# Three-branch attention with tokens on partitions: scores in two fp32r passes over stacked halves, probabilities as the stationary operand of the values' product, row sums divided out on the output

## The reference, cut to what matters

```python
def nsa_mixer(q, kc_raw, vc_raw, ks, vs, kw, vw, gates, pe, w1, w2, pos):
    q = rope(q), k_slc, k_win = rope(ks), rope(kw)
    p_cmp = safe_softmax(q @ k_cmp * 64 ** -0.5, compressed blocks that have ended)
    o_cmp = p_cmp @ v_cmp
    p = safe_softmax(q @ k_slc * 64 ** -0.5, mask);  o_slc = p @ v_slc
    p = safe_softmax(q @ k_win * 64 ** -0.5, mask);  o_win = p @ v_win
    return g[0] * o_cmp + g[1] * o_slc + g[2] * o_win
x = x + nsa_mixer(...) @ w_out
```

## Time and profile before

| | us |
|---|---|
| three runs | 4187.68, 4189.05, 4184.48; median 4187.68 |
| profiled execution, span (no other time of it is given) | 4191.9 |
| PE busy in the span | 3583.0 (85%) |
| PE weight loads | 2803.3 (67%) |
| DVE busy | 2293.2 (55%) |
| POOL busy | 1835.0 (44%) |
| ACT busy | 1449.5 (35%) |

### The profile page before, as it was taken

The page is one execution under the profiler, slowest core; times in us unless marked ns, Lnnn a source line. Parts: engine busy times, 40 slices in busy tenths (PEclk is TensorE's granted clock), DMA queues, the critical chain, the costliest instruction groups (busy, mean ns, idle before and its releaser), DMA issues. The chain is left out here.

```text
span 4191.9 us, 50533 instructions
## 1 busy us (share of the span) xinstructions
PE 3583.0 (85%) x16155; PEld 2803.3 (67%) x16159; DVE 2293.2 (55%) x3832; ACT 1449.5 (35%) x2631; POOL 1835.0 (44%) x986
## 2 busy tenths in 40 slices
PE   7778888745599999999998885889997779979997
PEld 4546576634488888888886653568776554457876
DVE  5976323887499999999995367421102326531101
ACT  4223332267633333333333232433212114433322
POOL 1521243178787888788883110134342200023432
PEclk9888999877799999999998897999998869999999
DMA  3121133012477777777772210123223130012321
GB/s 87 50 73 26 39 87 86 26 61 100 166 260 270 267 268 271 264 265 262 275 268 76 72 41 26 31 65 95 78 83 76 47 81 9 18 55 83 92 79 61
DMA packets 430765, 486.47 MB, mean 116 GB/s; under 512 B 61336, under 2 KB 373944, under 8 KB 412480
## 3 DMA queue, kind: packets, MB, share of 16 engines
q1 hardware_dynamic: 412224, 350.96, 27.8%
q0 software_dynamic: 18432, 134.23, 8.1%
HBM read 448.35 MB, written 29.36 MB: 114 GB/s over the span
## 5 line engine op out<-in xcount | busy, mean ns | idle before, releaser
L124 POOL TENSOR_TENSOR w_low<-w_ring,w_high 128x1024 fp32r<-128x1024 f32 (+2 forms) x264 | 650.4, 2471 | 1786.7 <-ACT w_high L119 1786.7
L129 PE MATMUL ps<-h_low,w_high 128*128 128x512 f32 x1600 | 657.3, 411 | 186.6 <-POOL w_low L124 133.1
L130 PE MATMUL ps<-h_high,w_high 128*128 128x512 f32 x1600 | 643.9, 402 | 0.0
L131 PE MATMUL ps<-h_high,w_low 128*128 128x512 f32 x1600 | 642.6, 402 | 0.0
L129 PEld LDWEIGHTS ps<-h_low,w_high 128*128 128x128 f32 x1600 | 309.5, 193 | 281.3 <-POOL w_low L124 148.6
L124 POOL TENSOR_TENSOR u_low<-w_ring,u_high 128x1024 fp32r<-128x1024 f32 x128 | 365.8, 2857 | 134.1 <-ACT u_high L119 133.6
L124 POOL TENSOR_TENSOR v_low<-v_raw,v_high 128x1024 fp32r<-128x1024 f32 x128 | 349.2, 2728 | 45.6 <-ACT v_high L119 45.6
L119 ACT ACTIVATE w_high<-w_ring 128x1024 fp32r<-128x1024 f32 (+2 forms) x264 | 263.1, 1012 | 301.5 <-PE ps L131 253.9
L130 PEld LDWEIGHTS ps<-h_high,w_high 128*128 128x128 f32 x1600 | 310.5, 194 | 72.9 <-issue 3.6
L131 PEld LDWEIGHTS ps<-h_high,w_low 128*128 128x128 f32 x1600 | 309.1, 193 | 73.5
L129 PE MATMUL ps<-h_low,u_high 128*128 128x384 f32 x1024 | 344.7, 337 | 6.5 <-POOL u_low L124 6.5
(11 more groups left out here) (395 smaller groups left out, 7063.7 us busy)
## 6 DMA issues: line engine op xcount, KB each, us to landing
w_ring<-in_peer_uT_dram SPq DMA_DIRECT2D x128, 512.0 KB, 5.2
v_raw<-in_peer_uv_dram SPq DMA_DIRECT2D x128, 512.0 KB, 4.3
peer_gates<-ring SPq DMA_DIRECT2D x12, 2048.0 KB, 6.2
gates<-peer_gates SPq DMA_DIRECT2D x32, 768.0 KB
w_ring<-in_ffn_w_gate_dram SPq DMA_DIRECT2D x44, 512.0 KB, 3.8
w_ring<-in_ffn_w_up_dram SPq DMA_DIRECT2D x44, 512.0 KB, 3.8
w_ring<-in_w_in_dram SPq DMA_DIRECT2D x36, 512.0 KB, 3.9
w_ring<-in_ffn_w_down_dram SPq DMA_DIRECT2D x32, 448.0 KB, 3.7
```

What stands on the lines that cost most here:

```text
L124: return eng.tensor_tensor(rounded(low), whole, high, ALU.subtract)
L129: nc.tensor.matmul(out, rounded(w_high), rounded(x_low), start=start, stop=False, **more)
L130: nc.tensor.matmul(out, rounded(w_high), rounded(x_high), start=False, stop=False, **more)
L131: return nc.tensor.matmul(out, rounded(w_low), rounded(x_high), start=False, stop=stop, **more)
```

## The change

It keeps what is computed and changes how, in four places.

`compressed` gets two more outputs: ACT makes 12 high halves (4 tiles of keys, 8 of queries, 128x512 each) at the head of its program in that stage, ahead of the copy of peT; POOL makes the 12 low halves behind its memset.

`nsa_attention` stacks halves on partitions: q's stack holds the 64 rows of the high half over the 64 rows of the low half of one head; the keys' two operands hold the high half twice, and the low half twice. A score is then two fp32r matmuls over 128 rows (all four products of halves). Staging takes two 64-partition copies for each of 8 q slots, 9 for each kind's keys and values, 2 for pc0 with vc, one for pc1: 37 in a turn instead of 11.

`attention_rows` replaces `attention` for this stage. Steps, lag, maxima, exps, masks, transposes and the split of copies over ACT (tiles 1, 3) and DVE (0, 2) stay. The probabilities are neither scaled nor gated. The transposes go through 3 banks in rotation. In `weigh` the transposed probabilities are stationary and 64 columns of values move: 10 matmuls a unit, and in kind 0 four more for the compressed branch, each kind into its own bank (6 and 7 by turns). A new `finish` on DVE, between the copy of tile 2 and the next step's maximum, does the reciprocal of the four row sums, the product with the gates, the scaling of the output [128, 4, 64], and its addition to the compressed part (kind 0) or to the rows so far (kind 1).

`project` gets `rows`: the output has tokens on partitions now, so PE transposes it, 4 transposes for each of 8 tiles into banks 4 to 7, and ACT and DVE take both halves from PSUM.

```diff
 def project(c, w, evacuate, ..., rows=None):
...
+    x_whole = (lambda k: whole[:, k, :]) if rows is None else (lambda k: c.ps[:, 4 + k % 4, :])
...
+            if rows is not None:
+                for k in range(KD):
+                    if k >= 4:
+                        pe.wait_ge(x_low, k - 3)
+                    for t in range(TT):
+                        tr = nc.tensor.transpose(c.ps[:, 4 + k % 4, t * P:(t + 1) * P], rows[:, t, k * P:(k + 1) * P], c.ident[:, :])
+                    tr.then_inc(x_turned, 1)
...
+                for k in range(x_tiles):
+                    if rows is not None:
+                        act.wait_ge(x_turned, k + 1)
+                    high_half(nc, rhs[0].high[:, k, :], x_whole(k)).then_inc(x_high, 1)
...
+def attention_rows(c, turns, units, staging, lag=3):
+    s_banks, pt_banks, out_banks = (0, 1, 2), (3, 4, 5), (6, 7)
...
+                def score(i, s):
...
+                    for x, (q, k) in enumerate(unit["scores"]):
+                        nc.tensor.matmul(c.ps[:, bank, 0:w], q[:, t * P:(t + 1) * P], k[:, 0:w], start=x == 0, stop=False)
...
+                def weigh(i, u):
+                    unit = units[u]
+                    for t in (act_tiles[-1], dve_tiles[-1]):
+                        moved(pe, i, TT * u + t)
+                    pe.wait_ge(o_read, i * n_units + (u + 1))
+                    for t in range(TT):
+                        tokens = slice(t * P, (t + 1) * P)
+                        for j in range(t + 1):
+                            mm = nc.tensor.matmul(out_of(u)[:, t, :], probsT[:, u % 2, j, tokens], unit["v"](j), start=j == 0, stop=j == t, skip_group_check=True)
+                        if "beside" in unit:
+                            weights, values = unit["beside"]
+                            mm = nc.tensor.matmul(out_of(u, 1)[:, t, :], weights[:, tokens], values, start=True, stop=True, skip_group_check=True)
+                    mm.then_inc(pv_done, 1)
...
+            @block.vector
...
+                    for s in range(n_steps + lag):
+                        if s < n_steps:
+                            u, t = steps[s]
+                            dve.wait_ge(scored, i * n_steps + (s + 1))
+                            nc.vector.tensor_reduce(top[...], c.ps[...], AX.X, ALU.max, negate=True).then_inc(topped, 1)
+                        if s >= lag and steps[s - lag][1] in dve_tiles:
+                            move(dve, i, s - lag, pt_dve, nc.vector.tensor_copy)
+                        if s >= lag and steps[s - lag][1] == 2 and steps[s - lag][0] >= 1:
+                            finish(steps[s - lag][0] - 1)
...
-def compressed(c, A, w, qT, kT, order, pcT, vcr):
+def compressed(c, A, w, qT, kT, order, pcT, vcr, q_halves, k_halves):
...
+        wholes = [(k_halves, x, kT[:, 2 + x, :]) for x in range(4)] + [(q_halves, x, qT[:, x, :]) for x in range(KD)]
...
             def _(pool):
                 nc.gpsimd.memset(hidden[:, :, :, :, :], 0.0).then_inc(padded, 1)
+                for n, (halves, x, whole) in enumerate(wholes):
+                    pool.wait_ge(split_high, n + 1)
+                    low_half(nc.gpsimd, halves.low[:, x, :], whole, halves.high[:, x, :]).then_inc(split_low, 1)
...
             def _(act):
+                for halves, x, whole in wholes:
+                    high_half(nc, halves.high[:, x, :], whole).then_inc(split_high, 1)
                 act.wait_ge(pe_turned, 1)
...
-def nsa_attention(c, qT, kT, vs, vw, order, pcT, vcr, oT):
+def nsa_attention(c, q_halves, k_halves, vs, vw, order, pcT, vcr, o_rows):
...
+        def q_stack(j, b):
+            return lambda i: [(q[j, b][HALF[x], :], q_halves[x][HALF[b], i * TILES + j, :]) for x in range(2)]
+
+        def kv(kind, buf):
+            return lambda i: [(k[kind, b][x][HALF[y], :], k_halves[x][HALF[b], i + 2 * kind, :])
+                              for b in range(2) for x in range(2) for y in range(2)] + [(v[kind][:, :, :], buf[:, :, bass.ds(i * P, P)])]
...
+            def finish(dve, i, out, beside, total):
...
+                nc.vector.reciprocal(gate, total).then_inc(turned, 1)
+                dve.wait_ge(turned, now)
+                nc.vector.tensor_tensor(gate, gate, order[...], ALU.mult).then_inc(gated, 1)
+                dve.wait_ge(gated, now)
+                nc.vector.tensor_tensor(one, out, gate.unsqueeze(2).to_broadcast([P, TT, NSA_D]), ALU.mult).then_inc(parted, 1)
+                dve.wait_ge(parted, now)
+                return nc.vector.tensor_tensor(dest, one, beside if kind == 0 else dest, ALU.add)
```

More of the change, by code:

```diff
@@ L337, in count, with project @@
         return False
-def project(c, w, evacuate, rhs=None, ahead=None, whole=None, before={}, after={}, norm=None):
+def project(c, w, evacuate, rhs=None, ahead=None, whole=None, before={}, after={}, norm=None, rows=None):
     nc = c.nc
@@ L353, in project @@
     mm_done, bank_free, high, low = (ctx.sem(n) for n in ("mm_done", "bank_free", "high", "low"))
-    x_high, x_low = ctx.sem("x_high"), ctx.sem("x_low")
+    x_turned, x_high, x_low = ctx.sem("x_turned"), ctx.sem("x_high"), ctx.sem("x_low")
     w_halves = c.halves(ctx, "w", [P, per_turn, max(w.kt) * P])
+    x_whole = (lambda k: whole[:, k, :]) if rows is None else (lambda k: c.ps[:, 4 + k % 4, :])
+    x_tiles = whole.shape[1] if whole is not None else KD if rows is not None else 0
     fresh = w.count(c)
@@ L414, in _ @@
                 before["pe"](pe)
-            if whole is not None:
-                pe.wait_ge(x_low, whole.shape[1])
+            if rows is not None:
[5 more added lines that the diff above has]
+                    tr.then_inc(x_turned, 1)
+            if x_tiles:
+                pe.wait_ge(x_low, x_tiles)
             def body(i):
@@ L447, in start @@
             def start():
-                if whole is not None:
-                    for k in range(whole.shape[1]):
-                        high_half(nc, rhs[0].high[:, k, :], whole[:, k, :]).then_inc(x_high, 1)
+                for k in range(x_tiles):
+                    if rows is not None:
+                        act.wait_ge(x_turned, k + 1)
+                    high_half(nc, rhs[0].high[:, k, :], x_whole(k)).then_inc(x_high, 1)
             if "act" not in evacuate:
@@ L491, in _ @@
                 before["dve"](dve)
-            if whole is not None:
-                for k in range(whole.shape[1]):
-                    dve.wait_ge(x_high, k + 1)
-                    low_half(nc.vector, rhs[0].low[:, k, :], whole[:, k, :], rhs[0].high[:, k, :]).then_inc(x_low, 1)
+            for k in range(x_tiles):
+                dve.wait_ge(x_high, k + 1)
+                low_half(nc.vector, rhs[0].low[:, k, :], x_whole(k), rhs[0].high[:, k, :]).then_inc(x_low, 1)
             if "dve" in evacuate:
@@ L530, in project_copy, with project_add @@
     project(c, w, {"act": act}, ahead=ahead, before=before, after=after, norm=norm)
-def project_add(c, w, dest, rhs, whole=None, ahead=None, before={}):
+def project_add(c, w, dest, rhs, whole=None, ahead=None, before={}, rows=None):
     nc = c.nc
@@ L541, in dve @@
             nc.vector.tensor_tensor(d, d, c.ps[:, b, :], ALU.add).then_inc(bank_free, w.parts)
-    project(c, w, {"dve": dve}, rhs, ahead, whole, before)
+    project(c, w, {"dve": dve}, rhs, ahead, whole, before, rows=rows)
 def project_swiglu(c, w, gain, dest, ahead=None):
@@ L2429, in odd_mix @@
         c.h = c.halves(ctx, "h", [P, KD, T])
[L2430 removed]
+        o_rows = ctx.sbuf("o_rows", [P, TT, KD, P])
         with c.stage() as ctx:
[L2432 to L2433 removed]
+            k_halves = c.halves(ctx, "k", [P, 4, T])
             vs, vw = (ctx.sbuf(n, [P, TT, GW]) for n in ("vs", "vw"))
@@ L2629, in head @@
-        def head(j, b, kind):
-            half = slice(64 * b, 64 * b + 64)
-            unit = dict(q=q[j][half, :], k=lambda i: k[kind][half, :], v=lambda x: v[kind][:, x, half], mask=None,
-                        slots=[f"q{j}", f"kv{kind}"] + ["pc0", f"pc{j // 2}"][:1 + j // 2] * (kind == 0),
-                        gate=lambda i, t: order[:, t, 1 + kind, bass.ds(i * (2 * TILES) + (2 * j + b), 1)],
-                        out=c.ps[half, 7, :], sum=c.ps[:, 7, :], first=kind == 0, last=kind == 1)
+        stat = ctx.sbuf("stat", [P, 2, TT])
@@ L2636, in head @@
             if kind == 0:
                 rows = slice(32 * (2 * (j % 2) + b), 32 * (2 * (j % 2) + b) + 32)
-                unit["add"], unit["add_to"] = vc[rows, :], lambda i: pc[j // 2][rows, :]
+                unit["beside"] = pc[j // 2][rows, :], vc[rows, :]
             return unit
-        attention(c, KD // TILES, [head(j, b, kind) for j in range(TILES) for b in range(2) for kind in range(2)], 1.0, staging,
-                  {4 * j + 3: (lambda i, j=j: tile_of(oT, i, TILES, j)) for j in range(TILES)})
+        attention_rows(c, KD // TILES, [head(n, kind) for n in range(len(heads)) for kind in range(2)], staging)
```

170 lines of the change are left out of this document (146 added, 24 removed).

## The result

| | before | after |
|---|---|---|
| median of the runs, us | 4188.4 (4 runs) | 4252.3 (4 runs, 4243.9 to 4252.9) |
| ratio | 1 | 1.0147 (1.0135 to 1.0160) |
| profiled span, us | 4191.9 | 4251.2 |

The change costs 64 us (1.5%). I forecast slower, and +145. The profiled execution of the kernel before lay 3.5 us above its median, so the two spans differ by 59.3.

A forecast was written before the change was run, and what follows sets the result against it. No engine bounds the whole kernel; PE, busy throughout attention, was taken to run it at 1.2 GHz. Attention +122, staging +11.8, compressed stage +5.6, projection +4.4, last finish +0.7 make +145, so 4333 us; 8-in-10 range 4205 to 4375.

The forecast's parts named there:

- rival D: Attention: clock alternates because some stretch of new scores or products raises it; half the excess over rival B, some 4270; chance 0.14.
- The step that failed: Attention: all of it at 1.2 GHz, a pair 23.3 us, 16 pairs 373 instead of 240 us.
- The window's values: Window unit's weighing: 10 products of 2 instructions, 0.213 us each, 4.27 us in all at 1.2 GHz.
- The four scores of a unit: Attention unit: four fp32r scores take 3.53 us at 1.2 GHz, was 5.47.
- The score of 128 columns: Narrowest score: priced like the plain product, 2x0.43 us; bounds for a pass 0.11 and 0.43.
- The compressed part: Selected unit: compressed product becomes 4 products of 2 instructions, 8x0.213 = 1.71 us.
- rival B: Attention: clock rises and stays, DVE's finish chain of 4.6 plus weighing 2.4 bounds a unit at 7.0 us: 4210; chance 0.13.
- the cover of the finish: Attention units: DVE's finish, 1.2 us, hidden because PE needs 6.5 us between weighings and the chain under 5.
- Staging: Ahead of attention: SP issues copies at 0.63 to 0.76 us each, vc now the 25th, first score +11.8 us.
- Compressed stage: Stage before attention: 12 high halves on ACT ahead of peT's copy, +5.6 us; low halves on POOL at nothing.
- Output projection: After attention: ACT's split of oT waits for PE's transposes, +4.4 us; the last finish adds +0.7.
- Rival C: Attention: clock high, finish slips in while PE weighs, PE decides; 35 saved, 22 given back: 4175; chance 0.08.

The follow-up runs named there:

- e10: Changed kernel with score passes over only the 64 high-half rows of q, products with q's low half left out: 4349.8 us, ratio 1.0382.
- e6: e4 with q padded by zeros, so the plain fp32 scores run over 128 rows: 4233.8 us, ratio 1.0107.
- e4: Changed kernel with scores and staging put back to the earlier plain fp32 form; values, finish and output stay new: 4387.8 us, ratio 1.0474.
- e9: Changed kernel with the selected unit's compressed products moved out of its value weighing, finish left in place: 4235.6 us, ratio 1.0108.
- e13: e9 plus eight unread fp32r matmuls of 256 columns in the idle time ahead of the window weighing: 4193.9 us, ratio 1.0014.
- e7: Changed kernel with staging copies issued from two queues, SP and POOL: 4251.8 us, ratio 1.0143.
- e5: e1 with the selected unit's compressed products also moved out of its value weighing: 4161.7 us, ratio 0.9935.
- e12: e5 with the copy order of e11 and ACT's high halves moved behind the copy of peT: 4142.1 us, ratio 0.9882.
- e11: Changed kernel with only SP's staging order altered, the first unit's slots first: 4243.9 us, ratio 1.0134.
- e3: Kernel before with only the new scores, their splitting and staging; values and output in the old form: 4179.2 us, ratio 0.9972.
- e1: Changed kernel with the finish one step later on DVE, behind the fourth tile's maximum: 4206.6 us, ratio 1.0038.

## Why the prediction was right or wrong

The direction and the range for 8 in 10 (4205 to 4375) held, the latter because D and B widened it; my own range, 4292 to 4375, and the size did not: +64 for +145. What happened is rival D, which I gave 0.14 and priced at 4270.

- **The step that failed** is "What is left, loads and short streams in turn, looks like the stretches that stayed at 0.50. I therefore take the whole new attention at 1.2 GHz." The stretch that I took for the likeness, has its scores over 64 rows ("64*128" in the row); the new scores are stacked over 128. e10 and e6 show that this is the difference: over 64 rows 4350 us, near my 4333, over 128 rows 4252; and e4's 4388 against e6's 4234. I had read the columns of the rows and not the rows of the operand. The one term was worth 16 x (23.3 - 17.65) = 90 us, more than the whole miss of 81. That e10 comes so near to 4333 is in part luck, as the next point shows.
- **The steps inside it**, read from e10, which is slow all through. The window's values cost 0.215 us an instruction, forecast 0.213. The four scores of a unit take 3.44 us (0.61, 0.73, 0.94, 1.16), forecast 3.53, by two errors that cancel. The score of 128 columns is 0.43 shorter than my 1.04 (0.85 and 0.19): its fp32r pass is one and not four, since the second pass begins 0.27, 0.39, 0.49 and 0.59 us behind the first for 128 to 512 columns, in even steps. I took the wrong end of my bounds, 0.43 where 0.11 was the other. The wide ones sum to 2.83 where I had 1.92 + 3 x 0.19 = 2.49, so their loads are not hidden as in the earlier trace rows. The compressed part was too cheap by 0.77 us (8 x 0.31 against 1.71). The price of 0.213 is near what these products take apart from the values (1.90 us for 8 at 1.2 GHz in e9, 3512.63 to 3514.53); what I had at nothing is the mixing.
- **The chain of rival B** held: 4.6 forecast, 4.61 measured, though its parts were off by up to 0.12 both ways, and the window unit at 2.4 GHz is 6.83 for B's 7.0. I named it as what would stand if the cover of the finish went. It went, for 24.5 us of waiting ahead of the selected weighings and 12.1 ahead of the window's. The nearest run to B, e13, took 4194 us for B's 4210, which left out the 5.9 us of waits for staging that my own sum has.
- **Why D's price was 18 too high.** "Half the excess over B" rested on my pair of 23.3. The pair that is slow all through is 24.2 (e10), so that was not too dear. But the measured one has the low clock for less than half of it: some 6.5 of 17.65 us in the pair above, in the selected weighing and the scores behind it.
- **Staging:** first score +12.0, forecast +11.8. The waits for the window keys were 3.7 and 3.6, forecast 2.6 and 1.7; the boundary 2.2, forecast 3.2. The mechanism was wrong in part: I took SP's issue as the limit, and two queues do not halve it (e7).
- **Compressed stage:** PE got peT 5.9 us later, forecast 5.6, but only +3.7 arrived at the stage's end, at a mean clock of 0.59 against 0.57. The 60.4 it is held against is the longer of the stage's two lengths (56.3 in e4); against the shorter one it is +7.8. What decides between the two was not tried.
- **Output projection:** from the end of the last product of values to the first of the projection 13.3 us against 9.5, +3.9, forecast 4.4 + 0.7.
- **Rival C** (faster, PE bound, 4175) describes e5 and e12 (4162 and 4142 us), whose finish stands elsewhere. Its saving of 1.07 us a unit on scores was 1.25 (0.41, 0.63, 0.84, 1.05 us from the narrowest to the widest before; 0.29, 0.35, 0.46, 0.58 after, at 2.4 GHz).

Left open: e11's 8 us are not all in its own place, as its compressed stage began 3.7 us earlier than in the changed kernel with no edit ahead of it. The same holds for 5.6 of the 20 us between e5 and e12 (3368.93 and 3363.29). What makes the clock fall behind the mixed weighings, the number of their products or the mixture of 32 and 128 rows, was not separated, since e5 and e9 changed both. The output projection's 4 us were not tried by themselves.

## What to carry to other kernels

When a change rewrites a matmul, compare the rows as well as the columns of the operands that are busy before and after: here the same products at the same count lay 154 us apart by whether their scores ran over 64 or 128 rows (e4, e6). Put a new epilogue on DVE behind the maximum that the next hand-over hangs on, even where the average says DVE is half idle, and don't mix products of 32 rows among those of 128: standing apart they were 1.05 us a pair cheaper, and with the late finish the clock held. A change that is slower as a whole can hold two good parts; undoing halves of it (e3, e4) and then moving two statements (e5) turned +64 into -28, and with the edges -47.

## What the runs showed of the hardware that I had not expected

- TensorE busy for 128 of 128 us at a granted clock of 0.50 (e10, 3462 to 3590 us), with score operands of 64 rows; over 128 rows it rose (0.82 in the same stretch of the changed kernel), and rows of zeros did as well (e6).
- An fp32r matmul of 128 columns runs in one pass, as those of 256 and more: 0.15 us from start to start at 2.4 GHz, where 256, 384 and 512 columns take 0.20, 0.26 and 0.32 (3510.47 to 3512.78 in the changed kernel).
- Products of 64 columns behind a 128x128 load take 0.11 us an instruction at 2.4 GHz and 0.215 at 1.2: 20 of them cost no more than 8 with 64-column weights and 128 to 512 moving columns. The same with 32 rows take 0.13 and 0.24 in a row of 8 by themselves (e12, e9), but 0.18 and 0.31 by twos among those of 128 rows (e1, e10).
- Copies within SBUF from two queues slowed each other, from 1.15 us for two copies to as much as 3.93, with the DMA engines 99% busy (e7, 3434 to 3444 us).
- Work that nobody reads made a kernel faster: 8 matmuls a pair took it from 4236 (e9) to 4194 us (e13), with the clock held in all but 2 stretches.
